# Two projections of a two-block layer as seven block products each, with head norms inside the key selection

## The chip, the cores and the metric

One core of one Trainium2 chip runs the kernel. The metric is device time in microseconds (us) of one execution. TensorE is called PE here, VectorE DVE, ScalarE ACT, GpSimd POOL, and the queue that issues most loads SP. They run side by side, and order between them is made by semaphores only.

## The reference, cut to what matters

Two transformer blocks run in sequence over 256 tokens of width 1024, all in float32. The change lies in the first attention of the first block.

```python
h = rms_norm(x, g_norm)
proj = h @ w_in                       # q_a, k_a, v_a, q_i, k_i, w_i, z_a, ... are column ranges of it
q_a = partial_rope(rms_norm(q_a.reshape(b, s, 8, 64), g_qn_a), cos_a, sin_a)   # k_a likewise
# dsa_attention(q_a, k_a, v_a, q_i, k_i, w_i):
dots  = einsum('bqhc,bsc->bhqs', q_i, k_i) * 64 ** -0.5
index = einsum('bhqs,bqh->bqs', relu(dots), w_i * 8 ** -0.5)      # causal
_, idx = lax.top_k(index, 64)         # each query keeps its 64 best keys
o_a = softmax(q_a k_a[idx] * 64 ** -0.5) v_a[idx]
```

Two more attentions (B and M), gates and an output projection follow, then the second block: two mixers, a cross attention, and a mixture of 32 experts whose weights are 201 MB.

## The kernel before

**Projections.** `h`, transposed, lies in `XT3` as 8 tiles of 128 rows by 256 tokens. The weights come in chunks of 512 columns (2 MB) from DRAM into three ring slots in turn, issued by SP when the last user of the slot is done. A chunk is multiplied in one of two ways. `project` (matmul on line 535) makes 16 matmuls 512 wide; each is two instructions in the trace, 32 for a chunk, and the result of both token tiles lies in one accumulator. `project_blocks` (lines 666 to 704, matmuls on lines 688 and 691) treats the chunk as a 2 by 2 block matrix and makes seven block products instead of eight (Strassen's scheme in Winograd's form): 28 matmuls 256 wide, 56 instructions. It needs four sums of weight blocks, which POOL makes (`weight_sums`, the `tensor_tensor` on line 1337, 16 steps of 128 by 256 for a chunk: 12 before the products, and four more once the second product is done), and four sums of `XT3`'s blocks, which POOL makes once, into `T_x`. DVE then joins the seven products (`combine`, lines 1897 to 1925) in four parts. Part k of the first three waits for product 2, 4 or 6; part 3 waits for product 7. The end of the third part frees the first accumulator, the end of the fourth part frees the second. In the kernel before, the chunks `mv`, `qi`, `qm`, the gates and most later ones are done so, while `qa`, `ka` and `va` (queries, keys and values of the first attention) go through `project`, and ACT copies their results out (`drain`, line 1458).

**Accumulators.** There are two, `ACC[0]` and `ACC[1]`, and every use takes the next one: use n waits until use n-2 has been freed (`acc`, line 495). `project` makes one use, `project_blocks` two, called low (products 1 to 4) and high (5 to 7).

**Order on PE** around the change: `qi`, `uq`, `ukv`, eight transposes, `qa`, `ka` (with the eight index score pairs of `dots`, line 783, one after each of its first eight matmuls), `va`, `za` (`project_t`, line 550), 16 transposes of `qa` and `ka`, `zb` with the first attention's steps in between, then `qm`.

**Order on DVE**: join `qi`; head norm of B's queries; head norm of B's keys (`norm_heads`: a reduce on line 1817, 12 small steps of a reciprocal root on lines 1767 to 1784, scale on 1826, gain on 1832); relu'd index scores times weights, added up (lines 2037 and 2039); mask (2047); the selection, eight rounds of `max` (2053) and `match_replace` (2056); two closing steps; then the head norm of `qa` and `ka` (`heads_normed` 4, called norm A here); then `silu_t` of `za` (line 1949), which waits for PE, and the attention.

**Order on POOL**: weight sums of `qi`; rope of the index queries; copies that join B's keys (1380, 1381), for which ACT waits to square them; rope of B's queries and keys (1322 to 1325) after B's key norm; rope of `qa` and `ka` after norm A; then the sums of `qm`.

**ACT** drains accumulators, squares heads for the norms, and takes the relu of the index scores. It may take pair n once DVE has added up pair n-2.

Of the kernel before, what the change touches and what calls it, by code (L numbers as in the profile page):

```python
# [20 lines left out]
ALU = mybir.AluOpType  # L21
# [5 lines left out]
S = 256  # L27
# [7 lines left out]
TOPK = 64  # L35
# [21 lines left out]
def two_block_layer(nc, A, out):  # L57
    ctx = ExitStack()
    with ctx:
# [126 lines left out]


        gate_chunks = [f"gate{n}{h}" for n in range(3) for h in range(2)]
        block_chunks = ["mv", "qi", "qm"] + gate_chunks + ["wout0", "wout1", "ckv0", "dq", "dk", "gv", "ckv1", "gg"]
        WS = slots[RING - 1]  # L190
        S_a, S_b = (WS[:, 1024 * i:1024 + 1024 * i].rearrange("p (k n) -> p k n", k=4) for i in range(2))
        T_x, T_mem2 = (t.rearrange("p (i k q) -> p i k q", i=4, k=4) for t in (WS[:, 2048:4096], R5[:, 2048:4096]))
# [220 lines left out]
        def keys_of(t):  # L413
            return P if t == 0 else S
# [79 lines left out]
        def _(pe):  # L494
# [20 lines left out]
            def project(name, lhs, k=KD, a=0, width=512, key=None, between=None, after=None, ready=None):  # L515


                if name != "mk":
                    wait_chunk(name)
                bank, full = acc(key or name)  # L520
                w = slot_of(name)
                for t in range(TT):
                    if t and between:
                        between()
                    for i in range(k):
                        if name == "mk":
                            if i % 4 == 0:
                                wait_drained(pe, ("mem", t, i // 4))
                            if t == 0 and i in (0, 2):
                                pe.wait_ge(first_landed[i // 2], 16)  # L530
                            elif (t, i) == (0, 4):
                                wait_chunk(name)
                        if ready and t == 0:
                            ready(i)
                        mm = nc.tensor.matmul(bank[:, t * 512:t * 512 + width], lhs[:, i, t * P:(t + 1) * P],  # L535
                                              w[:, i, a:a + width], start=(i == 0), stop=(i == k - 1))
                        if (t, i) == (TT - 1, k - 1):
                            mm.then_inc(full, 1)
                        if after:
                            after(t * k + i + 1, TT * k)  # L540
                last_job[name] = key or name
# [228 lines left out]
            for t in range(TT):  # L770
                turn(t, ("qi", t))
                turn(2 + t, ("ki", t))
            project("qa", XT3)
            for t in range(TT):
                wait_drained(pe, ("qi", t))
                wait_drained(pe, ("ki", t))
            def dots(n):
                t, h = n // 4, n % 4
                nk = keys_of(t)
                full = [aux(2 * (n % 2) + i, ("dots", n, i))[1] for i in range(2)]  # L780
                for i in range(2):
                    r = slice(64 * i, 64 * i + 64)
                    nc.tensor.matmul(AUX[2 * (n % 2) + i][:, 0:nk], QT4[r, h, t * P:(t + 1) * P], KIT[r, 0:nk],
                                     start=True, stop=True).then_inc(full[i], 1)

            project("ka", XT3, after=lambda done, total: dots(done - 1) if done <= 8 else None)
            project("va", XT3)
            project_t("za", XT3)
            pe.wait_ge(roped, 3)
            for t in range(TT):  # L790
# [488 lines left out]
        def _(pool):  # L1279
# [55 lines left out]
            def add_steps(out, a, b, op, counter, value):  # L1335
                for k in range(4):
                    ins = g.tensor_tensor(out[:, k, :], a[:, k, :], b[:, k, :], op)  # L1337
                ins.then_inc(counter, 1)
                pool.wait_ge(counter, value)

            def weight_sums(name):

                c = block_chunks.index(name)
                pool.wait_ge(slot_landed[slot_no[chunk_at[name]]], landed_value[chunk_at[name]])
                w = slot_of(name)
                w11, w12, w21, w22 = (w[:, 4 * j:4 * j + 4, 256 * i:256 * i + 256] for i in range(2) for j in range(2))
                if c:
                    pool.wait_ge(block_products, 3 * c - 1)
                add_steps(S_a, w21, w22, ALU.add, w_sums, 4 * c + 1)
                add_steps(S_b, S_a, w11, ALU.subtract, w_sums, 4 * c + 2)  # L1350
                add_steps(w21, w11, w21, ALU.subtract, w_sums, 4 * c + 3)
                pool.wait_ge(block_products, 3 * c + 1)
                add_steps(w12, w12, S_b, ALU.subtract, w_sums, 4 * c + 4)

            weight_sums("mv")
            for t in range(TT):
# [15 lines left out]
            for t in range(TT):  # L1372
                for i in range(2):
                    last = g.tensor_copy(EX[:, t * P + 64 * i:t * P + 64 * i + 64], PJ3[:, t, PJ_KI:PJ_KI + 64])
            last.then_inc(roped, 1)

            wait_drained(pool, "ukv0")
            wait_drained(pool, "ukv1")
            for t in range(TT):
                g.tensor_copy(KB[:, t, :, 0:64], KNB[:, t, :, :])  # L1380
                last = g.tensor_copy(KB[:, t, :, 64:96],
                                     PJ3[:, t, PJ_KR:PJ_KR + 32].unsqueeze(1).broadcast_to([P, 8, 32]))
            last.then_inc(kb_joined, 1)
            pool.wait_ge(heads_normed, 3)
            for t in range(TT):
                rope(heads(QB, t, 0, 8, 96), t, 64, 16, 1, 8)
                rope(KB[:, t, :, :], t, 64, 16, 1, 8)
            g.memset(SMALL[:, 72:73], 0.0).then_inc(roped, 1)
            pool.wait_ge(heads_normed, 4)
            for t in range(TT):  # L1390
                rope(heads(PJ3, t, PJ_QA, 16, 64), t, 0, 8, 2, 16)
# [36 lines left out]
        def _(act):  # L1428
# [25 lines left out]
            def drain(key, pairs):  # L1454

                bank = wait_full(act, key)
                for dst, src in pairs:
                    last = a_.activation(dst, src(bank), ACT.Copy)
                last.then_inc(free_sem(key), 1)

            def by_token(T3, c, width=512):
                return [(T3[:, t, c:c + width], lambda b, t=t: b[:, t * 512:t * 512 + width]) for t in range(TT)]
# [81 lines left out]
                drain(("ki", t), [(KIT[:, t * P:(t + 1) * P], lambda b: b[:, 0:P])])  # L1544
            act.wait_ge(kb_joined, 1)
            square_heads(R2[:, 0:1536], SQ[:, 0:1536], 96)
            drain("qa", by_token(PJ3, PJ_QA))
            for n in range(8):
                nk = keys_of(n // 4)
                if n >= 2:  # L1550
# [6 lines left out]
            wait_drained(act, "ka")  # L1557
            wait_drained(act, "qa")
            square_heads(PJ3[:, :, 0:1024], SQ[:, :].rearrange("p (t n) -> p t n", t=TT), 64)
            drain("va", by_token(PJ3, PJ_VA))  # L1560

            def tanh_of(key, dst, cols_=lambda b: b[:, :], done=None):

# [191 lines left out]
        def _(dve):  # L1755
# [3 lines left out]
            def link(ins):  # L1759
                steps[0] += 1  # L1760
                ins.then_inc(dve_steps, 1)
                dve.wait_ge(dve_steps, steps[0])
# [50 lines left out]
            def norm_heads(squares, groups, w, apply, n_gains):  # L1813

                sq_calls[0] += 1
                dve.wait_ge(squares_ready, sq_calls[0])
                v.tensor_reduce(MS[:, 0:groups], squares.rearrange("p (g w) -> p g w", g=groups), AX_X,
                                ALU.add).then_inc(squares_used, 1)
                dve.wait_ge(squares_used, sq_calls[0])
                rsqrt(groups, MS[:, 0:groups])  # L1820
                apply()
# [13 lines left out]
            def hv(ap, h):  # L1835
                return ap.rearrange("p (h w) -> p h w", h=h)
# [177 lines left out]
            def apply_heads(per_tile, gain, count=True):  # L2014

                for t in range(TT):
                    view, c = per_tile(t)
                    ins = scale_heads(view, c, view.shape[1])
                link(ins)
                for t in range(TT):  # L2020
                    view, c = per_tile(t)
                    ins = gain_heads(view, gain)
                ins.then_inc(heads_normed, 1)

            norm_heads(SQ[:, 0:1536], 16, 96, lambda: apply_heads(lambda t: (hv(QB[:, t, :], 8), 8 * t), GB_B), 1)
            norm_heads(SQ[:, 0:1536], 16, 96, lambda: apply_heads(lambda t: (KB[:, t, :, :], 8 * t), GB_B + 96), 1)

            for n in range(8):
                t = n // 4
# [18 lines left out]
            link(ins)  # L2048

            best = NW[:, 0:16].rearrange("p (t n) -> p t n", t=TT)  # L2050
            for k in range(TOPK // 8):
                for t in range(TT):
                    ins = v.max(best[:, t, :], IX3[:, t, 0:keys_of(t)])
                link(ins)
                for t in range(TT):
                    ins = v.match_replace(IX3[:, t, 0:keys_of(t)], best[:, t, :], IX3[:, t, 0:keys_of(t)], TAKEN)
                link(ins)
            for t in range(TT):
                nk = keys_of(t)
                ins = v.tensor_scalar(IX3[:, t, 0:nk], IX3[:, t, 0:nk], -2e38, NEG, ALU.is_gt, ALU.mult)  # L2060
            link(ins)
            for t in range(TT):
                nk = keys_of(t)
                ins = v.tensor_tensor(SEL3[:, t, 0:nk], IX3[:, t, 0:nk], causal[:, S - nk:S], ALU.add)
            link(ins)

            def apply_a(q, k, g0):
                def go():
# [14 lines left out]
                return go  # L2083

            norm_heads(SQ[:, :], 32, 64, apply_a(lambda t: hv(PJ3[:, t, 0:1024], 16), None, GB_A), 2)
            silu_t("za", ZT[:, 0:1024])
            attention("A", 0, 6)
            silu_t("zb", ZT[:, 1024:2048])
# [354 lines left out]
```

## Time and profile before

| | |
|---|---|
| median of 3 runs | 1104.6 us (1104.5 to 1105.12) |
| the profiled execution | 1104.28 us, of which the span of its trace 1102.5 us |
| PE busy | 921.5 us, 84% |
| DVE busy | 405.2 us, 37% |
| POOL busy | 244.4 us, 22% |
| ACT busy | 166.9 us, 15% |
| bytes moved | 290.38 MB, 263 GB/s over the span |

The profile is a page about one execution and a trace of it. Times in a trace count from the start of the span. Engines count as busy only with real work, and busy time is modelled for PE's pipelined matmuls, so the spacing of two starts is a better measure than a duration. A trace row of a timeline merges like instructions: start, time from the first start to the last end, line, operation, shapes, count, and in brackets how long the engine had been idle and what ended that.

### The profile page before, as it was taken

To read this page: it belongs to the slowest core of one execution; us is meant where nothing else is said; L and a number is where in the kernel's file an instruction comes from. 1 tells how busy PE (TensorE), PEld (TensorE's weight loads), DVE (VectorE), ACT (ScalarE), POOL (GpSimd) and SP (SyncE) were. 2 spreads that over 40 slices of the span, in tenths; PEclk is the share of its full clock that TensorE was granted. 3 is DMA by queue.
4 is the path that set the end of the run, shared out by engine and by line. 5 is a ranking of instruction groups with operands and counts; after the bars stand their busy time and mean duration, and the time that the engine had idled before them with its cause. 6 is when DMAs were issued, how large, how long until landed. Compare 5 with 4: busy or idle time off the path is not lost.

```text
span 1102.5 us, 12492 instructions
## 1 busy us (share of the span) xinstructions
PE 921.5 (84%) x5006; PEld 569.7 (52%) x5006; DVE 405.2 (37%) x994; ACT 166.9 (15%) x372; POOL 244.4 (22%) x366
## 2 busy tenths in 40 slices
PE   6999999999999999999999998757465566473757
PEld 3774487889999878864445653222222122131312
DVE  4736836663223746868445433010101001010101
ACT  2113223441001013013302230000000000000000
POOL 4442143044654958930000000000000000000000
PEclk9999999999999999999999999878878878687879
DMA  7645342232445344524419649999999999999996
GB/s 286 168 146 191 121 153 78 77 130 100 157 168 207 105 171 169 201 87 153 153 68 346 252 173 428 427 429 427 428 428 427 427 428 427 428 429 427 427 416 272
DMA packets 64328, 290.38 MB, mean 263 GB/s; under 512 B 9031, under 2 KB 11918, under 8 KB 51726
## 3 DMA queue, kind: packets, MB, share of 16 engines
q1 hardware_dynamic: 57840, 205.13, 48.6%
q10 hardware_dynamic: 6430, 84.44, 18.1%
q8 instruction: 41, 0.67, 0.3%
q14 instruction: 17, 0.14, 0.0%
HBM read 288.51 MB, written 1.05 MB: 263 GB/s over the span
## 4 chain that ended last, share of the span: by engine, by line
PE 62%; DMA 26%; DVE 6%; issue 2%; another core or an unknown queue 2%; ACT 2%; ACTq 0%; SPq 0%; DVEq 0%
DMA ring<-in_w_e_up_dram 12%; PE ACC L535 10%; PE ACC L691 10%; DMA BIG<-in_w_e_up_dram 9%; PE ACC L550 9%; PE PAIR L1086 8%; PE ACC L688 7%; PE ACC L574 5%; DMA PJ<-in_w_e_up_dram 4%; PE ACC L977 3%; PE PAIR L585 2%; PE PAIR L1117 2%; PE PAIR L662 1%; PE PAIR L639 1%
## 5 line engine op out<-in xcount | busy, mean ns | idle before, releaser
L1337 POOL TENSOR_TENSOR ring<-ring 128x256 f32<-128x256 f32 x272 | 205.3, 785 | 167.3 <-PE ACC L688 75.5
L1086 PE MATMUL PAIR<-ring,R 128*32 128x512 f32 x400 | 130.4, 708 | 41.2 <-DMA BIG<-in_w_e_up_dram 20.8
L550 PE MATMUL ACC<-BIG,ring 128*128 128x256 f32 (+1 forms) x464 | 103.8, 381 | 0.6 <-DVE R L1921 0.6
L550 PEld LDWEIGHTS ACC<-BIG,ring 128*128 128x128 f32 (+1 forms) x464 | 85.4, 187 | 15.5 <-issue 3.1
L2378 DVE SCALAR_TENSOR_TENSOR GB<-GB,PAIR 128x512 f32<-128x512 f32 x8 | 5.5, 688 | 231.8 <-ACT GB L1728 231.8
L1086 PE MATMUL PAIR<-BIG,R 128*32 128x512 f32 x176 | 62.8, 727 | 22.1 <-DMA PJ<-in_w_e_up_dram 22.1
L1086 PE MATMUL PAIR<-R 128*32 128x512 f32 x176 | 59.7, 695 | 25.0 <-DMA ring<-in_w_e_up_dram 12.5
L1117 PE MATMUL PAIR<-ring,BIG 128*32 128x512 f32 x160 | 64.5, 747 | 18.0 <-DMA R<-in_w_e_down_dram 12.4
L535 PE MATMUL ACC<-ring,BIG 128*128 128x512 f32 (+2 forms) x192 | 78.1, 559 | 0.5 <-DVE R L2214 0.5
L1086 PE MATMUL PAIR<-SQE,R 128*32 128x512 f32 x112 | 61.4, 711 | 17.0 <-DMA ring<-in_w_e_up_dram 10.7
L1086 PEld LDWEIGHTS PAIR<-ring,R 128*32 128x32 f32 x400 | 30.9, 128 | 73.2 <-issue 73.2
L691 PE MATMUL ACC<-ring 128*128 128x256 f32 x288 | 64.9, 381 | 1.9 <-ACT R L1512 1.0
L535 PE MATMUL ACC<-ring,R 128*128 128x512 f32 (+1 forms) x136 | 59.1, 584 | 0.7 <-DVE R L2007 0.4
L691 PEld LDWEIGHTS ACC<-ring 128*128 128x128 f32 x288 | 54.3, 190 | 10.4 <-issue 1.8
L1117 PE MATMUL PAIR<-PJ,BIG 128*32 128x512 f32 x128 | 46.7, 746 | 14.4 <-DMA ring<-in_w_e_down_dram 14.4
L2380 DVE SCALAR_TENSOR_TENSOR GB<-GB,PAIR 128x512 f32<-128x512 f32 x8 | 8.4, 1052 | 131.8 <-PE PAIR L1086 131.8
L574 PE MATMUL ACC<-ring,BIG 128*128 128x512 f32 x128 | 55.8, 592 | 0.0
L1086 PE MATMUL PAIR<-PJ,R 128*32 128x512 f32 x160 | 50.8, 698 | 5.7 <-DMA ring<-in_w_e_up_dram 5.0
L535 PEld LDWEIGHTS ACC<-ring,BIG 128*128 128x128 f32 x192 | 35.6, 190 | 35.2 <-issue 27.0
L688 PE MATMUL ACC<-ring 128*128 128x128 f32 x384 | 45.1, 276 | 0.0
L688 PEld LDWEIGHTS ACC<-ring 128*128 128x128 f32 x384 | 44.1, 192 | 0.7 <-issue 0.5
L691 PE MATMUL ACC<-ring,R 128*128 128x256 f32 x184 | 40.9, 379 | 0.0
(346 smaller groups left out, 1402.5 us busy)
## 6 DMA issues: line engine op xcount, KB each, us to landing
ring<-in_w_in_dram SPq DMA_DIRECT2D x20, 2048.0 KB, 7.9
ring<-in_w_e_gate_dram SPq DMA_DIRECT2D x8, 2048.0 KB, 40.1
ring<-in_w_e_up_dram SPq DMA_DIRECT2D x6, 2048.0 KB, 41.1
ring<-in_w_e_gate_dram ACTq DMA_DIRECT2D x6, 2048.0 KB, 26.5
ring<-in_w_e_down_dram SPq DMA_DIRECT2D x5, 2048.0 KB, 39.1
ring<-in_w_e_up_dram ACTq DMA_DIRECT2D x5, 2048.0 KB, 20.9
ring<-in_w_ckv_dram SPq DMA_DIRECT2D x4, 2048.0 KB, 8.0
BIG<-in_w_e_down_dram SPq DMA_DIRECT2D x4, 2048.0 KB, 22.9
```

What stands on the lines that cost most here:

```text
L535: mm = nc.tensor.matmul(bank[:, t * 512:t * 512 + width], lhs[:, i, t * P:(t + 1) * P], w[:, i, a:a + width], start=(i == 0), stop=(i == k ...
L550: mm = nc.tensor.matmul(bank[0:m, j * S:(j + 1) * S], w[:, i, a + j * P:a + j * P + m], rhs[:, i, :], start=(i == 0), stop=(i == k - 1))
L574: mm = nc.tensor.matmul(bank[:, c:c + 512], lhs[:, i, t * P:(t + 1) * P], w[:, i, :], start=(i == order[0]), stop=(i == order[-1]))
L585: mm = nc.tensor.transpose(bank[0:src.shape[1], j * P:(j + 1) * P], src, ident[:, :])
L639: mm = nc.tensor.transpose(bank[:, (j * heads + i) * P:(j * heads + i + 1) * P], e[:, i, j * P:(j + 1) * P], ident[:, :])
L662: mm = nc.tensor.matmul(bank[:, d * 256:(d + 1) * 256], value(j, h, d), p[:, j * 256:(j + 1) * 256], start=first, stop=last)
L688: mm = nc.tensor.matmul(bank[:, j * P:(j + 1) * P], left[:, k, j * P:(j + 1) * P], right[:, k, :], start=(k == 0), stop=(k == 3))
L691: mm = nc.tensor.matmul(bank, right[:, k, :], left[:, k, :], start=(k == 0), stop=(k == 3))
L977: mm = nc.tensor.matmul(ACC[t][:, h * 512:(h + 1) * 512], XT3[:, i, t * P:(t + 1) * P], slot_of(f"wco{h}")[:, i, :], start=False, stop=Fal ...
L1086: mm = nc.tensor.matmul(bank[r, :], M_xt[:, k, r], w[e][:, k, :], start=(k == 0), stop=(k == KD - 1))
L1117: mm = nc.tensor.matmul(AUX[2 + h][r, :], M_hidt[:, k, r], w[e][:, k, h * 512:(h + 1) * 512], start=(k == 0), stop=(k == 3))
L1337: ins = g.tensor_tensor(out[:, k, :], a[:, k, :], b[:, k, :], op)
```

## The change

`qa` and `va` are made by `project_blocks`. ACT's two drains of them go. POOL makes their weight sums: 12 steps for `qa` after the rope of the index queries, the other four after the copies that join B's keys; all 16 for `va` after the rope of B's queries and keys, ahead of that of `qa` and `ka`. DVE joins `qa` in two pieces, parts 0 to 2 between the two norms of B and part 3 after them. Norm A moves from behind the selection to behind its third round. Parts 0 to 2 of `va` come after norm A, part 3 after the sixth round. The index scores start four matmuls later within `ka`.

```diff
-        block_chunks = ["mv", "qi", "qm"] + gate_chunks + [...]
+        block_chunks = ["mv", "qi", "qa", "va", "qm"] + gate_chunks + [...]
 # PE
-            project("qa", XT3)
+            project_blocks("qa", XT3, T_x, x0_sums)
-            project("ka", XT3, after=lambda done, total: dots(done - 1) if done <= 8 else None)
-            project("va", XT3)
+            project("ka", XT3, after=lambda done, total: dots(done - 5) if 5 <= done <= 12 else None)
+            project_blocks("va", XT3, T_x, x0_sums)
 # POOL: weight_sums is split into first_sums (12 steps) and last_sum (4 steps)
             last.then_inc(roped, 1)
+            first_sums("qa")
...
             last.then_inc(kb_joined, 1)
+            last_sum("qa")
             pool.wait_ge(heads_normed, 3)
...
             g.memset(SMALL[:, 72:73], 0.0).then_inc(roped, 1)
+            weight_sums("va")
             pool.wait_ge(heads_normed, 4)
 # ACT
-            drain("qa", by_token(PJ3, PJ_QA))
-            drain("va", by_token(PJ3, PJ_VA))
 # DVE
             norm_heads(... QB ...)
+            combine("qa", by_rows(PJ3, PJ_QA), range(3))
             norm_heads(... KB ...)
+            combine("qa", by_rows(PJ3, PJ_QA), range(3, 4))
...
-            for k in range(TOPK // 8):      # the eight rounds, then the two closing steps, then norm A
+            select(range(0, 3))
             norm_heads(SQ[:, :], 32, 64, apply_a(lambda t: hv(PJ3[:, t, 0:1024], 16), None, GB_A), 2)
+            combine("va", by_rows(PJ3, PJ_VA), range(3))
+            select(range(3, 6))
+            combine("va", by_rows(PJ3, PJ_VA), range(3, 4))
+            select(range(6, TOPK // 8))
+            # the two closing steps
             silu_t("za", ZT[:, 0:1024])
```

## Rows read from the trace of the kernel before

**Rows 1.** The page: busy time, share of the span, instructions
```profile
PE 921.5 (84%) x5006; PEld 569.7 (52%) x5006; DVE 405.2 (37%) x994; ACT 166.9 (15%) x372; POOL 244.4 (22%) x366
```
**Rows 2.** A window of the end: us, busy per engine (instructions), granted clock, DMA share, GB/s
```profile
700.00:1102.00 402.00, 246.79 (x1651) 90.19 (x1649) 34.22 (x70) 15.82 (x29) 0.00 (x0) 0.81 0.99 417
```
**Rows 3.** Timeline of PE: qi's products, qa, the last dots, va, za
```profile
66.30 7.07 PE L691 MATMUL ACC<-ring 128*128 128x256 f32 x32
...
92.35 14.76 PE L535 MATMUL ACC<-ring,BIG 128*128 128x512 f32 x34
...
118.01 0.70 PE L783 MATMUL PAIR<-R 64*128 64x256 f32 x4
118.65 20.87 PE L535 MATMUL ACC<-ring,BIG 128*128 128x512 f32 x48
139.35 13.98 PE L550 MATMUL ACC<-BIG,ring 128*128 128x256 f32 x64
```
**Rows 4.** Timeline of DVE: joining qi, from part 0 to part 3
```profile
71.41 0.42 DVE L1913 COPY PJ<-ACC 128x256 f32<-128x256 f32 x1
...
73.41 0.42 DVE L1919 TENSOR_TENSOR PJ<-ACC,PJ 128x256 f32<-128x256 f32 x1 [0.33 <-PE ACC L691]
...
74.54 1.68 DVE L2007 TENSOR_TENSOR R<-PAIR,GC 128x384 f32<-128x384 f32 x4
76.23 0.42 DVE L1924 TENSOR_TENSOR PJ<-ACC,PJ 128x256 f32<-128x256 f32 x1
```
**Rows 5.** Timeline of DVE: B's key norm, score sums, mask, first round
```profile
97.70 1.75 DVE L1817 TENSOR_REDUCE MS<-SQE 128x16 f32<-128x1536 f32 x1 [2.36 <-ACT SQE L1452]
...
120.33 0.63 DVE L2047 TENSOR_TENSOR BIG<-BIG,MASKS 128x128 f32<-128x128 f32 x2
120.99 0.62 DVE L2053 MAX8 NW<-BIG 128x8 f32<-128x128 f32 x2
...
122.43 0.62 DVE L2053 MAX8 NW<-BIG 128x8 f32<-128x128 f32 x2
```
**Rows 6.** Timeline of DVE: norm A, first and last steps, and what comes next
```profile
133.63 2.29 DVE L1817 TENSOR_REDUCE MS<-SQE 128x32 f32<-128x2048 f32 x1
135.95 0.18 DVE L1767 TENSOR_SCALAR NW<-MS 128x32 f32<-128x32 f32 x1
...
138.63 2.36 DVE L1826 TENSOR_TENSOR PJ<-PJ,RS 128x1024 f32<-128x1024 f32 x2
141.03 2.50 DVE L1832 TENSOR_TENSOR PJ<-PJ,GB 128x512 f32<-128x512 f32 x4
154.42 1.22 DVE L1949 SCALAR_TENSOR_TENSOR BIG<-BIG,ACC 128x1024 f32<-128x1024 f32 x1 [10.90 <-ACT BIG L1565]
```
**Rows 7.** Timelines of POOL and DVE: a root step and a join beside sums
```profile
66.61 2.77 POOL L1337 TENSOR_TENSOR ring<-ring 128x256 f32<-128x256 f32 x4 [4.43 <-PE ACC L691]
...
67.39 0.65 DVE L1784 SCALAR_TENSOR_TENSOR NW<-NW 128x4 f32<-128x4 f32 x1
...
187.14 8.49 POOL L1337 TENSOR_TENSOR ring<-ring 128x256 f32<-128x256 f32 x12 [3.11 <-PE ACC L691]
...
191.92 0.42 DVE L1920 TENSOR_TENSOR PJ<-PJ,ACC 128x256 f32<-128x256 f32 x1
```
**Rows 8.** Timeline of POOL: rope of B, first step to last
```profile
105.78 0.73 POOL L1322 TENSOR_TENSOR BIG<-R,PJ 128x256 f32<-128x256 f32 x1 [9.62 <-DVE R L1832]
...
115.19 0.64 POOL L1325 TENSOR_TENSOR R<-BIG 128x128 f32<-128x128 f32 x1
```
**Rows 9.** Windows of 1 us, columns as in rows 2: PE stopped and started again
```profile
684.00:685.00 1.00, 0.40 (x4) 0.17 (x2) 1.00 (x3) 0.38 (x1) 0.00 (x0) 1.00 0.90 377
...
687.00:688.00 1.00, 0.00 (x0) 0.00 (x0) 0.00 (x0) 0.00 (x0) 0.00 (x0) 0.78 1.08 459
...
689.00:690.00 1.00, 0.02 (x4) 0.05 (x5) 0.00 (x0) 0.00 (x0) 0.00 (x0) 0.50 0.97 410
...
694.00:695.00 1.00, 1.00 (x12) 0.36 (x8) 0.00 (x0) 0.00 (x0) 0.00 (x0) 0.80 0.93 385
```

More of the change, by code:

```diff
@@ L188, in two_block_layer @@
         gate_chunks = [f"gate{n}{h}" for n in range(3) for h in range(2)]
-        block_chunks = ["mv", "qi", "qm"] + gate_chunks + ["wout0", "wout1", "ckv0", "dq", "dk", "gv", "ckv1", "gg"]
+        block_chunks = ["mv", "qi", "qa", "va", "qm"] + gate_chunks + ["wout0", "wout1", "ckv0", "dq", "dk", "gv", "ckv1", "gg"]
         WS = slots[RING - 1]
@@ L1339, in add_steps, with first_sums @@
                 pool.wait_ge(counter, value)
-            def weight_sums(name):
+            def first_sums(name):
                 c = block_chunks.index(name)
@@ L1351, in weight_sums, with last_sum @@
                 add_steps(w21, w11, w21, ALU.subtract, w_sums, 4 * c + 3)
+            def last_sum(name):
+                c = block_chunks.index(name)
+                w12 = slot_of(name)[:, 4:8, 0:256]
                 pool.wait_ge(block_products, 3 * c + 1)
                 add_steps(w12, w12, S_b, ALU.subtract, w_sums, 4 * c + 4)
+            def weight_sums(name):
+                first_sums(name)
+                last_sum(name)
             weight_sums("mv")
@@ L2050, in _, with select @@
             best = NW[:, 0:16].rearrange("p (t n) -> p t n", t=TT)
-            for k in range(TOPK // 8):
[L2052 to L2065, printed above, removed]
+            def select(rounds):
+                for k in rounds:
+                    for t in range(TT):
+                        ins = v.max(best[:, t, :], IX3[:, t, 0:keys_of(t)])
+                    link(ins)
+                    for t in range(TT):
+                        ins = v.match_replace(IX3[:, t, 0:keys_of(t)], best[:, t, :], IX3[:, t, 0:keys_of(t)], TAKEN)
+                    link(ins)
+            select(range(0, 3))
             def apply_a(q, k, g0):
@@ L2085, in _ @@
             norm_heads(SQ[:, :], 32, 64, apply_a(lambda t: hv(PJ3[:, t, 0:1024], 16), None, GB_A), 2)
+            combine("va", by_rows(PJ3, PJ_VA), range(3))
+            select(range(3, 6))
+            combine("va", by_rows(PJ3, PJ_VA), range(3, 4))
+            select(range(6, TOPK // 8))
+            for t in range(TT):
+                nk = keys_of(t)
+                ins = v.tensor_scalar(IX3[:, t, 0:nk], IX3[:, t, 0:nk], -2e38, NEG, ALU.is_gt, ALU.mult)
+            link(ins)
+            for t in range(TT):
+                nk = keys_of(t)
+                ins = v.tensor_tensor(SEL3[:, t, 0:nk], IX3[:, t, 0:nk], causal[:, S - nk:S], ALU.add)
+            link(ins)
             silu_t("za", ZT[:, 0:1024])
```

## The prediction

> **What bounds the kernel now.** I read the page first, then the windows, then the timelines of PE, DVE and POOL between 60 and 165 us. PE is busy for 84% of the span, DVE for 37%, POOL for 22% [rows 1]. From 700 us on the DMA engines are 99% busy, streaming expert weights [rows 2]. That stream starts when PE's chain has freed the buffers, so a microsecond won or lost on PE at 100 us should reach the end whole. Around the change PE runs without a gap: `qa` starts at 92.35, the last pair of index scores ends at 118.71, `za` starts at 139.35 [rows 3]. DVE has ended norm A at 143.53 and then idles 10.9 us until `za` is there [rows 6]. So PE bounds here, and DVE's slack is not needed by PE until the transposes after `za`.
>
> **What PE gains.** A plain chunk is 32 instructions. 48 of them fill 118.65 to 139.35, 0.431 us each, so 13.8 us a chunk [rows 3]. A block product chunk is 56 instructions. 32 of them take 7.07 us, tail included, so 6.91 us by starts, 0.216 us each, and the chunk takes 12.1 us [rows 3]. Two chunks: 3.4 us less on PE. If nothing waits the profiled 1104.3 us become 1100.9. ACT's two dropped drains are off the path.
>
> **What waits instead.** Count accumulator uses from 0 at `mk`: `qa` becomes uses 11 and 12, `ka` 13, `va` 14 and 15, `za` 16. `za` needs the accumulator of use 14, the low half of `va`, and DVE frees that by parts 0 to 2 of joining `va`. These stand in DVE's order behind norm A, and norm A behind three rounds of the selection. Before, `za` needed only `ka` drained by ACT. The question is when DVE gets there.
>
> 1. `qa` starts at 92.35 as before. Its sixth product, for which part 2 of the join waits, ends 48 instructions later, near 102.9. Queued behind that wait is B's key norm, which began at 97.70 [rows 5]. DVE then needs 1.1 us for part 2 (73.41 to 74.54 [rows 4]) and is at 104.0. The key norm takes 8.0 us: it ran from 97.70 [rows 5] until its gain released POOL, which started at 105.78 [rows 8]: 112.0. Part 3 takes 0.46 (76.23's row [rows 4], with its link): 112.5.
> 2. `ka` starts when `qa` ends, 92.35 + 12.1 = 104.4, against 106.15 before (92.35 + 13.8). With its scores it took 19.4 us, since `va`'s 13.8 before 139.35 leave 125.55. The last score pair ended at 118.71, 12.56 us after `ka`'s start, and now comes four matmuls (3.45 us) later: 120.4. The mask began 1.62 us after the last pair [rows 3, 5]: 122.0 now. DVE's own backlog, about 9 us of work from 112.5, ends at about the same time, so I take 122.3. The mask takes 0.66 us, a round 1.44 (120.99 to 122.43 [rows 5]), three rounds 4.3: 127.3. ACT has squared the heads by then (`ka` ends at 123.8, then about 3 us).
> 3. Norm A takes 9.9 us (133.63 to 143.53 [rows 6]): 137.2. Parts 0 to 2 take 2.8 us (71.41 to 74.54 less a wait of 0.33 [rows 4]): `za` could start at 140.0.
>
> PE is done with `va` at 104.4 + 19.4 + 12.1 = 135.9. So it stands idle for 4.1 us even with every DVE step at its old price, and the 3.4 us gained have turned into 0.65 us lost (140.0 against 139.35).
>
> **POOL's new work beside DVE.** Four small root steps beside weight sums started 0.68 us apart from 66.72 on (one of the four stands, 0.65 long [rows 7]), while alone the 12 steps from 135.95 to 138.63 are 0.22 apart [rows 6]. POOL itself was not slowed (2.77 us for four steps). A join step with only one input in SBUF kept its 0.42 beside sums [rows 7]. All 12 root steps of a norm are of this small kind. There are two places.
> - 12 steps for `qa`: the weights land about 84.1 and the steps end near 92.6 (8.49 us for 12 [rows 7]), over the root of B's query norm. This costs up to 3 us, hidden: DVE waits for `qa`'s sixth product until 102.9 anyhow. The copies for B's keys start within a microsecond of before. Were that cover gone, the 3 us would come through whole. The four later steps fit before product 7 starts.
> - 16 steps for `va`: they stand behind the rope of B, which starts when the key norm ends, 112.0, and takes 10.2 us (105.78 to 115.83 and a closing step of 0.1 [rows 8]): 122.2. Twelve steps at 8.5 us and four at 2.8 end at 133.5, at the worst spacing of the trace near 135. Norm A's root runs from 129.6 (127.3 and the reduce of 2.3). Until 133.5 it gets some six steps done at 0.68, the other six at 0.22: 2.7 us more, 3.5 if POOL ends at 135. I take 3.0. `va`'s own products get their sums in time (first at 125.1, wanted at 127.3); small delays of them would hide in PE's wait.
>
> `za` then starts at 143.0: 3.65 us later than before, after 7.1 us of idle PE. The rope of `qa` and `ka` on POOL (4.9 us) and the second half of the selection run under `za` (14 us); moving them costs nothing.
>
> **The clock.** In the trace PE stopped at 684.4 us, its granted clock fell from 2.4 to 1.2 GHz about 3 us later, stayed there when it started again at 689.98, and rose at about 694.4 [rows 9]. A stop of 7 us should do the same to `za`: some 3 to 6 us at half speed, of which half is lost, 1.5 to 3. I take 2.2, as in those rows. Should the clock not fall, it is 0.
>
> The sum: 1104.28 + 3.65 + 2.2 = 1110.1 for a profiled execution. The median of the runs lies 0.3 above the profiled one, so 1110.4.
>
> **What no row shows.** No `max` or `match_replace` ran beside POOL. Its cost in this company lies between nothing and the 0.45 more of a small step. At the upper end three rounds of 18 instructions take 8 us more, but then norm A runs after POOL is done and saves its 3: 5 us more in all. I take nothing, the end that the join step of rows 7 stands for: like it, each reads one tensor from SBUF. The Trainium skill ("VectorE: DVE Perf Modes", on two Vector instructions with no wait between them) counts the match instructions as one input each, and "SBUF — State Buffer" (practical consequences of the shared port) lets one-input instructions outside the two-port modes run free; by it the 5 us are 0. No run here shows it yet.
>
> **Rivals.**
> - *The joins are not late.* PE keeps its 3.4 us: 1101.2. For it speaks that DVE is 63% idle over the span; against it that DVE's steps from 102.9 to 140.0 are a chain each link of which has a row. It needs norm A and the join done 4 us sooner than their old durations allow. 7%.
> - *Late, but mildly.* POOL and DVE do not meet in norm A (sums over sooner, or steps that interleave), and a stop of 4 us brings the clock down for a short while only or not at all: +0.3 to +2.9, 1104.9 to 1107.5, middle 1105.9. 15%.
> - *Selection slowed by POOL*, as bounded above: 1115.4. It decides if a round takes 2.5 us or more instead of 1.44. 8%.
> - *Forecast*: `za` waits for the join of `va`, with both surcharges: 1110.4, own range 1107.5 to 1113.5. 70%.
>
> The range of 8 in 10 reaches from 1105.6 to 1114: part of the mild case, all of the forecast. A measurement of this kernel tells about 0.2% (2.2 us) from no change. Faster has the first rival, 0.07. Same (1102.4 to 1106.8) has most of the mild one, 0.12. Slower has the rest, 0.81.
>
> **What the profile after should show.** PE's stop in front of line 550 at about 136, some 7 us long, ended by DVE's join of `va`; no stop of note between 92 and 136. `qa` 12.1 us long. B's key norm at 104.0, first `max` at 123. Root steps of norm A at 0.65 us each while POOL is on line 1337, 0.2 after. The granted clock at 0.50 when `za` starts. The rest of the trace moved by one constant, about 6 us, up to the weight stream. The prediction is wrong if `za` starts with `va`'s last product, or if the clock stays at 1.00 through the stop (then about 1108.2), or if a later stage gives the delay back.

## The result

| | before | after |
|---|---|---|
| median | 1104.55 us (4 runs, 1103.96 to 1105.12) | 1111.25 us (4 runs, 1110.14 to 1112.16) |
| ratio to before | | 1.0061, 95% interval 1.0048 to 1.0073 |
| profiled execution, span | 1104.28, 1102.5 us | 1110.6, 1108.8 us |

The change makes the kernel 0.6% slower. The forecast was 1110.4 us with a range of 1105.6 to 1114. Two projections with an eighth of the matrix work taken out cost 6.7 us more, and the profile after shows where they go. First PE's timeline. It answers [rows 3]:

```profile
92.25 3.62 PE L691 MATMUL ACC<-ring,BIG 128*128 128x256 f32 x16
95.70 7.07 PE L691 MATMUL ACC<-ring 128*128 128x256 f32 x32
102.61 1.89 PE L691 MATMUL ACC<-ring,BIG 128*128 128x256 f32 x8
104.33 4.45 PE L535 MATMUL ACC<-ring,BIG 128*128 128x512 f32 x10
...
119.69 0.70 PE L783 MATMUL PAIR<-R 64*128 64x256 f32 x4
120.33 3.70 PE L535 MATMUL ACC<-ring,BIG 128*128 128x512 f32 x8
123.86 3.62 PE L691 MATMUL ACC<-ring,BIG 128*128 128x256 f32 x16
127.32 3.62 PE L691 MATMUL ACC<-ring 128*128 128x256 f32 x16
131.67 3.69 PE L691 MATMUL ACC<-ring 128*128 128x256 f32 x16 [0.73 <-issue]
135.20 1.89 PE L691 MATMUL ACC<-ring,BIG 128*128 128x256 f32 x8
143.63 15.76 PE L550 MATMUL ACC<-BIG,ring 128*128 128x256 f32 x64 [6.55 <-DVE PJ L1930]
159.23 1.91 PE L585 MATMUL PAIR<-ident,PJ 128*128 128x128 f32 x16
```

`qa` runs from 92.25 to 104.3, 12.1 us, and `va`'s products are done at 137.1. Then PE stands still for 6.55 us until `za` starts at 143.63, 4.3 us later than before. What releases it is line 1930 on DVE, the last operation of part 2 of the join of `va`. `za` itself takes 15.76 us instead of 13.98. The transposes behind it start at 159.23 instead of 153.16 (before), so 6.1 us are lost here, and the span is 6.3 longer.

DVE's timeline after shows what it did meanwhile. It answers [rows 5, 6]:

```profile
102.81 0.42 DVE L1928 TENSOR_TENSOR PJ<-ACC,PJ 128x256 f32<-128x256 f32 x1 [1.96 <-PE ACC L691]
...
103.94 1.74 DVE L1826 TENSOR_REDUCE MS<-SQE 128x16 f32<-128x1536 f32 x1
...
117.99 4.96 DVE L2050 SCALAR_TENSOR_TENSOR BIG<-SQE,SMALL,BIG 128x256 f32<-128x256 f32 x7
122.98 1.57 DVE L2058 TENSOR_TENSOR BIG<-BIG,MASKS 128x128 f32<-128x128 f32 x2
124.59 0.62 DVE L2065 MAX8 NW<-BIG 128x8 f32<-128x128 f32 x2
...
126.03 0.62 DVE L2065 MAX8 NW<-BIG 128x8 f32<-128x128 f32 x2
...
128.91 2.29 DVE L1826 TENSOR_REDUCE MS<-SQE 128x32 f32<-128x2048 f32 x1
131.23 0.38 DVE L1776 TENSOR_SCALAR NW<-MS 128x32 f32<-128x32 f32 x1
131.64 0.18 DVE L1777 TENSOR_SCALAR NWI<-NW 128x32 int32<-128x32 int32 x1
131.86 0.59 DVE L1778 TENSOR_SCALAR NW<-NWI 128x32 int32<-128x32 int32 x1
132.48 0.66 DVE L1787 TENSOR_TENSOR NW<-NW 128x32 f32<-128x32 f32 x1
133.17 0.65 DVE L1788 SCALAR_TENSOR_TENSOR NW<-NW 128x32 f32<-128x32 f32 x1
133.85 0.65 DVE L1793 SCALAR_TENSOR_TENSOR NW<-NW 128x32 f32<-128x32 f32 x1
134.54 0.19 DVE L1787 TENSOR_TENSOR NW<-NW 128x32 f32<-128x32 f32 x1
...
138.29 2.50 DVE L1841 TENSOR_TENSOR PJ<-PJ,GB 128x512 f32<-128x512 f32 x4
140.70 0.42 DVE L1922 COPY PJ<-ACC 128x256 f32<-128x256 f32 x1
...
143.07 0.42 DVE L1930 TENSOR_TENSOR PJ<-ACC,PJ 128x256 f32<-128x256 f32 x1
```

B's key norm starts at 103.94, behind the wait for `qa`'s sixth product. From there DVE works without a pause of note to 143.49, and the join of `va` is the last thing in the row. Norm A's root has 12 steps. Six of them start while POOL's sums run, and four of these six take 0.59 to 0.66 us (the other two 0.38 and 0.18); the six behind them take 0.19 each. POOL's row (its timeline after):

```profile
122.82 11.63 POOL L1337 TENSOR_TENSOR ring<-ring 128x256 f32<-128x256 f32 x16
```

The sums end at 134.45, and the next root step, at 134.54, is short.

### The profile page after: what moved, and what is told of

Same layout as the page of the kernel before. It is cut to its first block, busy times and chain, and to the rows that moved or that the text cites. A ratio compares the mean times of both kernels' runs of the same rounds, so it can differ in the third digit from the quotient of the medians.

```text
span 1108.8 us, 12645 instructions
## 1 busy us (share of the span) xinstructions
PE 918.6 (83%) x5054; PEld 579.9 (52%) x5054; DVE 421.3 (38%) x1010; ACT 164.9 (15%) x368; POOL 268.3 (24%) x398
## 3 DMA queue, kind: packets, MB, share of 16 engines
HBM read 288.51 MB, written 1.05 MB: 261 GB/s over the span
## 4 chain that ended last, share of the span: by engine, by line
PE 57%; DMA 27%; DVE 10%; issue 2%; ACT 2%; another core or an unknown queue 1%; ACTq 0%; SPq 0%; DVEq 0%
PE ACC L691 11%; DMA PJ<-in_w_e_down_dram 10%; PE ACC L550 9%; DMA PJ<-in_w_e_up_dram 9%; PE ACC L688 7%; PE ACC L535 6%; PE ACC L574 5%; PE PAIR L1086 5%; DMA ring<-in_w_e_down_dram 4%; PE PAIR L1117 4%; DMA ring<-in_w_e_up_dram 4%; PE ACC L977 2%; PE PAIR L585 2%; PE PAIR L662 1%
## 5 line engine op out<-in xcount | busy, mean ns | idle before, releaser
L1337 POOL TENSOR_TENSOR ring<-ring 128x256 f32<-128x256 f32 x304 | 230.2, 788 | 179.8 <-PE ACC L688 76.4
L691 PE MATMUL ACC<-ring 128*128 128x256 f32 x352 | 79.3, 381 | 3.1 <-issue 1.7
L691 PEld LDWEIGHTS ACC<-ring 128*128 128x128 f32 x352 | 66.4, 190 | 13.6 <-issue 2.9
L535 PE MATMUL ACC<-ring,BIG 128*128 128x512 f32 (+2 forms) x128 | 50.6, 542 | 0.4 <-DVE R L2233 0.4
L691 PE MATMUL ACC<-ring,BIG 128*128 128x256 f32 x192 | 44.8, 382 | 0.2 <-ACT BIG L1634 0.2
L688 PEld LDWEIGHTS ACC<-ring 128*128 128x128 f32 x384 | 44.1, 192 | 0.7 <-issue 0.5
```

The costliest lines, as they stand in the source:

```text
L688: mm = nc.tensor.matmul(bank[:, j * P:(j + 1) * P], left[:, k, j * P:(j + 1) * P], right[:, k, :], start=(k == 0), stop=(k == 3))
L691: mm = nc.tensor.matmul(bank, right[:, k, :], left[:, k, :], start=(k == 0), stop=(k == 3))
```

## The experiments

The theory on record says: `za` waits for `va`'s join because norm A stands ahead of it on DVE, POOL's sums make norm A longer, and the stop costs clock. All ratios below are to the kernel before.

### The join ahead of norm A

```diff
             select(range(0, 3))
-            norm_heads(SQ[:, :], 32, 64, apply_a(...), 2)
-            combine("va", by_rows(PJ3, PJ_VA), range(3))
             select(range(3, 6))
+            combine("va", by_rows(PJ3, PJ_VA), range(3))
+            norm_heads(SQ[:, :], 32, 64, apply_a(...), 2)
             combine("va", by_rows(PJ3, PJ_VA), range(3, 4))
```

> The changed kernel with one thing moved on DVE: rounds 3 to 5 of the selection, then parts 0 to 2 of joining va, and only then norm A. Theory (za waits for the join because norm A stands ahead of it): in the trace after, the join can follow the sixth round at 133.2 us and its part 2 ends near 136.5, before va's last product (137.1), so za starts near 137.1 instead of 143.6, PE has no stop, and the clock stays at 2.4 GHz. Norm A then runs from 136.5 beside an idle POOL, so its root steps are 0.22 us apart and it takes 9.9 us, to 146.5; the rope takes 4.9, to 151.4, about when za ends (150.9), so up to 0.6 us of wait there. Time: about 1.8 us under the kernel before, 1102.7, and 8 us under the changed kernel. Rival (the cost lies in the block products themselves, on PE or in POOL's sums, wherever norm A stands): as slow as the changed kernel within 2 us, 1109 to 1112.

Measured: 1102.91 us, ratio 0.9987 (0.9978 to 0.9996). PE's timeline of this kernel:

```profile
131.76 3.69 PE L691 MATMUL ACC<-ring 128*128 128x256 f32 x16 [0.73 <-issue]
135.29 1.89 PE L691 MATMUL ACC<-ring,BIG 128*128 128x256 f32 x8
137.02 13.98 PE L550 MATMUL ACC<-BIG,ring 128*128 128x256 f32 x64
151.77 1.97 PE L585 MATMUL PAIR<-ident,PJ 128*128 128x128 f32 x16 [0.78 <-POOL SMALL L1403]
```

The stop is gone with the same work on every engine. `za` follows `va`'s last product, and takes 13.98 us. Against the changed kernel the order of two items on DVE is worth some 8 us. The rival, that the block products cost by themselves, is out. The price forecast for the rope's wait, up to 0.6 us, was 0.78.

### PE kept busy through the stop

```diff
             project_blocks("va", XT3, T_x, x0_sums)
+            for i in range(2):
+                wait_drained(pe, ("dots", 6, i))
+            for _ in range(26):
+                nc.tensor.matmul(AUX[0][:, :], zeros_h[:, :], ..., start=True, stop=True)
```

> The changed kernel, with 26 matmuls of zeros (bf16, 512 wide, 0.216 us each, 5.6 us together) put on PE between va and za, into a bank that is free there. They lie inside PE's stop of 6.5 us, so za still starts at about 143.6. Theory (1.8 of the 6.3 us come from the clock, which fell to 1.2 GHz after the stop and stayed so for 3.5 us of za): the granted clock stays at 1.00 from 130 to 160 us, za's 64 instructions take 13.98 us instead of 15.76, and the kernel is 1.8 us faster than the changed one, 1109.4. Rival (za is long for another reason, such as late weights or DVE and POOL traffic): za stays at 15.8 us and the time at 1111.2.

Measured: 1109.1 us, ratio 1.0047 (1.0034 to 1.006). PE's timeline:

```profile
136.85 5.78 PE L791 MATMUL PAIR<-ones_h,zeros_h 128*128 128x512 bf16 x26
143.56 14.05 PE L550 MATMUL ACC<-BIG,ring 128*128 128x256 f32 x64 [0.93 <-DVE PJ L1935]
```

and two windows of 1 us, columns as in rows 2, first of the changed kernel, then of this one:

```profile
146.00:147.00 1.00, 1.00 (x4) 0.82 (x3) 0.93 (x4) 0.00 (x0) 1.00 (x2) 0.50 0.00 0
```

```profile
146.00:147.00 1.00, 1.00 (x6) 0.89 (x5) 0.93 (x5) 0.00 (x0) 1.00 (x2) 1.00 0.00 0
```

`za` starts at the same time, the granted clock stays at 2.4 GHz where it had been 1.2, and `za` is 1.7 us shorter. 5.8 us of useless matmuls make the kernel about 1.5 us faster (1.0047 against 1.0061, with intervals that overlap; the trace is the stronger evidence). So the clock's share of the loss is 1.7 to 1.8 us.

### Fewer sums on POOL

```diff
             def add_steps(out, a, b, op, counter, value):
-                for k in range(4):
+                for k in range(1 if 13 <= value <= 16 and counter is w_sums else 4):
```

This kernel leaves out three of the four steps of each of `va`'s sums, so its values of `va` are not the reference's, and its whole time may differ for that too. The stretch up to `za` is what counts.

> The changed kernel with three of four steps of va's weight sums left out on POOL (4 instead of 16), so that va's values are not those of the reference. POOL is done with them near 126 us instead of 134.5, before norm A's root. Theory (a small DVE step waits out a POOL step): norm A's root steps go back from up to 0.68 to 0.22 us apart, norm A takes 9.9 us instead of 11.8, the join of va ends about 1.9 us earlier, and za starts near 141.5 (PE's stop about 4.5 us, the clock still falls). Rival (POOL has nothing to do with it): norm A keeps 11.8 us and za starts at 143.6. The time over the whole may differ by more than that, since other values of va can change the routing of the experts; the stretch up to za is what counts.

Measured: 1108.61 us, ratio 1.0043 (1.0028 to 1.0057). DVE's timeline and PE's:

```profile
122.45 1.05 DVE L2058 TENSOR_TENSOR BIG<-BIG,MASKS 128x128 f32<-128x128 f32 x2
...
130.17 0.18 DVE L1776 TENSOR_SCALAR NW<-MS 128x32 f32<-128x32 f32 x1
...
132.63 0.19 DVE L1793 SCALAR_TENSOR_TENSOR RS<-NW 128x32 f32<-128x32 f32 x1
```

```profile
140.60 16.21 PE L550 MATMUL ACC<-BIG,ring 128*128 128x256 f32 x64 [5.01 <-DVE PJ L1930]
```

All 12 root steps are short now: 2.65 us from 130.17 to 132.82, against 4.63 from 131.23 to 135.86 in the changed kernel. Norm A takes 9.8 us, instead of 11.8. `za` starts at 140.60, 0.9 us earlier than expected: the mask, too, had waited for POOL (1.05 us now, 1.57 in the changed kernel, 0.63 before), and PE's scores were already 0.5 us earlier in this execution. The mask's 0.5 and the root's 2.0 are what this edit takes away of POOL's share, 2.5 us beside a stop of 6.55. PE still stops, for 5 us, and `za` still runs slow (16.21 us), so taking POOL's part away cures nothing by itself.

### qa alone

`va` is plain again, drained by ACT, without sums and joins; the rest is as in the changed kernel.

```diff
-            project_blocks("va", XT3, T_x, x0_sums)
+            project("va", XT3)
...
-            weight_sums("va")
-            combine("va", by_rows(PJ3, PJ_VA), range(3))
-            combine("va", by_rows(PJ3, PJ_VA), range(3, 4))
+            drain("va", by_token(PJ3, PJ_VA))
```

> The changed kernel with va as before: a plain product, drained by ACT, no sums of it on POOL and no joins on DVE. qa stays as block products, the norm stays inside the selection. Then za needs only ka's accumulator, which ACT drains at 125. Theory (qa's part is sound and its join is hidden; the loss comes from va's join alone): PE runs without a stop from 92 to za, which starts near 137.7, 1.7 us earlier than before, and the kernel takes 1102.9. Rival (qa's join already holds up PE or the index scores, or the extra DVE work costs by itself): no faster than the kernel before, 1104.5 or more.

Measured: 1102.86 us, ratio 0.9989 (0.998 to 0.9997). `za` starts at 137.46 with no stop (before: 139.35), and the transposes at 151.28 (before: 153.16), 1.9 us earlier. `qa`'s join is hidden as forecast, and so is the time by which POOL lengthens B's query norm. That is more than the 3 us of the forecast: the norm took 8.5 us before (86.87 to 95.34) and takes 12.5 here (86.63 to 99.13). The root pays 3.6 of it, and the gain step the rest, since `qa`'s last four sums run beside it (2.77 us instead of 2.31). In the changed kernel 1.96 us of DVE's wait for `qa`'s sixth product were left to cover it. The whole gains 1.2 us, not 1.7; the missing part is within the interval.

### The norm's move alone

The kernel before, with norm A behind the third round and nothing else changed.

```diff
+            select(range(0, 3))
             norm_heads(SQ[:, :], 32, 64, apply_a(...), 2)
+            select(range(3, TOPK // 8))
+            close_selection()
```

> The kernel before with one part of the change: norm A behind the third round of the selection instead of behind the eighth; no block products, no sums, no joins are added. Theory (the move is free while nothing behind norm A is wanted by PE before za ends): DVE does the same work in another order and ends it at the same 143.5 us, PE runs through, and the time is that of the kernel before, 1104, within 0.1%. Rival (the move brings or costs time by itself, since POOL's rope comes 7 us earlier and meets the last rounds): a difference of 1 us or more, 1103 or less or 1105 or more.

Measured: 1103.79 us, ratio 1.0003 (0.9994 to 1.0012). The move costs and brings nothing. DVE waits 3.67 us there for ACT's squares, so it ends this work at 147.1 and not at the 143.5 expected, but `za` starts at 139.37 as before.

### The norm last

The join-first kernel with norm A behind the whole selection, its old place.

```diff
             combine("va", by_rows(PJ3, PJ_VA), range(3))
-            norm_heads(SQ[:, :], 32, 64, apply_a(...), 2)
             combine("va", by_rows(PJ3, PJ_VA), range(3, 4))
             select(range(6, TOPK // 8))
...
+            norm_heads(SQ[:, :], 32, 64, apply_a(...), 2)
```

> The join-first kernel with norm A back behind the whole selection, where the kernel before had it. Theory: za still starts near 137.1 with no stop, but norm A ends near 151 and the rope near 156, while za ends at 150.9, so the stop of about 5 us stands ahead of the transposes now, and the clock falls again: the transposes start near 156 against 153.2 before, zb runs at half speed for some 3 us, and the time is 4 to 4.5 us above the kernel before, 1108.3. Rival (only the join's place matters, the norm's does not): as the join-first kernel, 1102.9.

Measured: 1110.1 us, ratio 1.0058 (1.0042 to 1.0073). PE's timeline:

```profile
136.78 13.98 PE L550 MATMUL ACC<-BIG,ring 128*128 128x256 f32 x64
156.48 3.52 PE L585 MATMUL PAIR<-ident,PJ 128*128 128x128 f32 x16 [5.73 <-POOL SMALL L1403]
159.84 5.35 PE L550 MATMUL ACC<-BIG,ring 128*128 128x256 f32 x24
```

The stop moves behind `za`, as forecast, and the transposes take 3.52 us instead of 1.91 at half clock. So DVE's order has two deadlines: the join by 137, norm A with its rope by about 151. The changed kernel misses the first, this one the second. The loss is 6.1 us by the medians, where 4 to 4.5 were expected. In the trace it is 4.9 us at line 688 (281.21 against 276.28 before): 3.3 from the later start of the transposes and 1.6 from their half clock. It is still 4.9 at the last expert products, and 5.2 between the two profiled executions (1109.44 against 1104.28). So nothing arises later in the trace; the rest lies between single executions and the median of only four, and its cause stays open.

### Both remaining waits taken out

```diff
 # DVE
-            select(range(3, 6))
+            select(range(3, 4))
+            v.tensor_reduce(MS[:, 0:32], ...)          # norm A's reduce
             combine("va", by_rows(PJ3, PJ_VA), range(3))
-            norm_heads(SQ[:, :], 32, 64, apply_a(...), 2)
+            rsqrt(32, MS[:, 0:32]); apply_a(...)()      # norm A's root and scaling
             combine("va", by_rows(PJ3, PJ_VA), range(3, 4))
-            select(range(6, TOPK // 8))
+            select(range(4, TOPK // 8))
 # POOL
-            pool.wait_ge(heads_normed, 3)
+            pool.wait_ge(heads_normed, 2)               # rope of B's queries
+            pool.wait_ge(heads_normed, 3)               # rope of B's keys, then va's sums
```

> The kernel of the join ahead of norm A, with what its trace still shows as lost taken out: the norm's reduce stands ahead of the join (four rounds, reduce, join of parts 0 to 2, root and scaling, part 3, four rounds), so that the rope of qa and ka is done 3 us earlier, and POOL ropes B's queries right after their own norm instead of behind the key norm, so that va's sums start 5 us earlier. Theory: the waits of 0.73 us (for va's third sum) and 0.78 us (for the rope) go, va ends near 136.4, za starts there or up to 0.4 later, the transposes follow it without a wait at about 150.2, and all of the 3.4 us of the block products are kept: 1.5 us faster than the join-first kernel, ratio to the kernel before 0.997, about 1100.7. Rival (the two waits only move, for instance into the closing steps of the selection or to DVE's score sums, which now have va's sums beside them): no better than the join-first kernel, ratio 0.9985 or more.

Measured: 1101.87 us, ratio 0.9978 (0.9969 to 0.9987). PE's timeline:

```profile
127.09 7.07 PE L691 MATMUL ACC<-ring 128*128 128x256 f32 x32
134.00 1.89 PE L691 MATMUL ACC<-ring,BIG 128*128 128x256 f32 x8
136.40 14.05 PE L550 MATMUL ACC<-BIG,ring 128*128 128x256 f32 x64 [0.51 <-DVE PJ L1932]
150.29 1.91 PE L585 MATMUL PAIR<-ident,PJ 128*128 128x128 f32 x16
```

Both waits are gone. 0.5 us is new in front of `za`, a part of what the rival said: the score sums have `va`'s weight sums beside them now and take 6.03 us for the last seven steps, instead of 4.96, so the join ends later than `va`. Still, the transposes start at 150.29, 2.9 us earlier than before and where they were expected. The time is 2.4 us under the kernel before and 9 us under the changed one; it is the fastest of the kernels here. It falls 0.8 us short of the ratio expected (0.997), at the edge of the interval.

## Why the prediction was right

**The gain on PE.** Forecast 3.4 us; `va` ended at 137.1 instead of the 135.9 forecast. 0.73 us are a wait inside it that I had ruled out. I had checked the first sum only. The third had no slack in my own numbers: done at 122.2 + 8.5 = 130.7, wanted 32 instructions into `va`, at 123.8 + 6.9 = 130.7. POOL's sums started 0.6 later than the 122.2 forecast (the rope took 10.7 us beside a busy DVE, not 10.2), the twelfth step ended at 131.57, and PE went on at 131.67. The wait hid in the stop, as the text had said it would, but it is real once the stop is gone, as the join-first kernel shows. Most of the other 0.4 us are no wait either: my sum went by starts, and at both stops the tail of the last instruction comes on top (0.17 us each, as 3.62 stands for 16 instructions that start over 3.45).

**The chain on DVE**, against the forecast:

| | forecast | after |
|---|---|---|
| B's key norm starts | 104.0 | 103.94 |
| score sums end | 122.3 | 122.95 |
| first `max` | 123.0 | 124.59 |
| three rounds | 4.3 | 4.3 |
| norm A | 12.9 (9.9 and 3.0) | 11.8 |
| join, parts 0 to 2 | 2.8 | 2.8 |
| `za` starts | 143.0 | 143.63 |

The term that was mis-sized is POOL's company, in its place more than in its size. I priced it for norm A alone, 3.0 us. The mask, two additions with both inputs in SBUF, paid 0.9 of it (1.57 us; 0.63 in the kernel with `qa` alone, where no sums run). The root paid 2.0 (4.63 instead of 2.65): it met 3.2 us of POOL's sums, not the 3.9 forecast, and its six steps there started 0.55 apart, not 0.68. That is 2.9 together. That the total came out at the 3.0 forecast is luck: an unpriced surcharge on the mask made up for a smaller one on the root.

The 0.6 us by which `za` started later than forecast come from the score sums. I had put DVE's backlog at "about 9 us of work from 112.5"; it took 10.7 (112.28 to 122.95, and with `qa` alone 112.15 to 122.84). Here, too, POOL was the company, with the rope of B: the steps of 256 columns take 0.71 us each beside it (4.96 for seven), where before, with POOL idle, they took 0.50 (the kernel before, a row of its DVE timeline):

```profile
117.61 1.00 DVE L2039 SCALAR_TENSOR_TENSOR BIG<-SQE,SMALL,BIG 128x256 f32<-128x256 f32 x2 [0.68 <-ACT SQE L1554]
```

The surcharge belongs to a stretch of time and to the operations in it.

**What no row had shown.** The rounds took 1.44 us beside POOL's sums (124.59 to 126.03), as alone [rows 5], so the lower bound of 0 was the right one. By the Trainium skill ("VectorE: DVE Perf Modes", on two Vector instructions with no wait between them) each match instruction has one input. No trace counts inputs, and the page's line does not name `max`; but the price of 0 that the prediction drew from it is what the trace shows for both, 1.44 us a round with and without company. The third rival is out.

**The clock.** Forecast 2.2 us, 1.5 to 3 as range; 1.78 in the trace (15.76 less 13.98), 1.7 by the kernel that kept PE busy. The windows after, of 1 us:

```profile
139.00:140.00 1.00, 0.00 (x0) 0.00 (x0) 1.00 (x2) 0.00 (x0) 0.00 (x0) 1.00 0.94 336
...
141.00:142.00 1.00, 0.00 (x0) 0.00 (x0) 0.93 (x4) 0.00 (x0) 1.00 (x2) 0.50 1.07 416
...
147.00:148.00 1.00, 1.00 (x5) 0.85 (x5) 0.96 (x5) 0.00 (x0) 1.00 (x3) 0.95 0.00 0
```

PE stopped at 137.1, the clock fell between 140 and 141, and rose again at 147, 3.5 us after the restart. That was 4.4 in [rows 9], hence the smaller loss. A shorter stop does not mean a smaller loss behind it. In the kernel with fewer sums PE stopped for 5.01 us only; its clock fell between 138 and 139, but stayed at 1.2 GHz for 4.4 us after the restart at 140.60, and `za` took 2.2 us more than 13.98:

```profile
144.00:145.00 1.00, 1.00 (x4) 0.73 (x4) 0.97 (x4) 0.00 (x0) 1.00 (x2) 0.51 0.00 0
145.00:146.00 1.00, 1.00 (x6) 0.90 (x5) 0.93 (x5) 0.00 (x0) 1.00 (x2) 1.00 0.00 0
```

**To the end of the kernel.** The forecast had 5.85 us at this point, 3.65 and 2.2; the trace has 4.28 and 1.78, together 6.1, so the two misses went opposite ways. 6.1 us at the transposes became 6.3 in the span and 6.7 in the medians. That the shift arrives whole was right for the changed kernel; for the small gains it holds only within about 1 us (1.9 us earlier at the transposes of the kernel with `qa` alone, 1.2 in the ratio). The tail from the first expert product on took 437.4 us before and 437.1 after, but 439.8 in the profiled execution of the fastest kernel. There PE was 2.8 us ahead of the kernel before at 645 and 0.45 ahead at the last expert product; at 1103.49 us it was also the slowest of that kernel's 11 executions. So one profile does not decide about a microsecond.

**The rivals.** "Not late" and "mildly late" failed for the same reason: with every step at its old price the join ends at 140.0, and the surcharges are facts. Without most of POOL's part PE still stopped for 5 us and the clock still fell and stayed low behind the restart, 4.4 us instead of 3.5 (the kernel with fewer sums, 1108.61 us), so the mild case ended nearer to the forecast than its 1104.9 to 1107.5.

## What to carry to other kernels

Before an accumulator is used twice as often, write down for each later user which engine now frees its bank, and everything that stands ahead of the freeing operation in that engine's queue; an engine that is busy 37% of the time can still be late where it counts. Place each item by its own deadline: here the join had to be done by 137 us and the norm with its rope by 151, and the order of just these two decided between 0.6% lost and 0.1% gained (0.2% with two small shifts more). And work added to POOL must be charged to every DVE operation of a slowed kind that runs in the same stretch, not only to the one that first comes to mind. Here these were operations with two inputs in SBUF, and `tensor_scalar` steps with one.

## What the runs showed of the hardware

- Beside POOL's two-input steps (0.69 to 0.73 us each) a small DVE step takes up to 0.66 us instead of 0.19, a mask of two additions 1.57 instead of 0.63. One input is no protection for `tensor_scalar`: in norm A's root two such steps took 0.38 and 0.59 us instead of 0.18, and the one between them 0.18. `max` and `match_replace` (1.44 us a round) and a reduce of 2048 columns (2.29 us) keep their times.
- It goes both ways: POOL's last four sums of `qa` took 4.59 us beside DVE's scaling and gain of 768 columns a step. The last four of `va` took 2.79 in the fastest kernel, beside rounds of the selection.
- After a stop of 6.55 us the granted clock was 1.2 GHz for the first 3.5 us of work, which cost 1.8 us; zero matmuls filling all but 0.93 us of the stop kept it at 2.4 GHz. After stops of 5.01 us (fewer sums) and 5.73 us (the norm last) the clock was at 1.2 GHz as well, and the work behind cost 2.2 and 1.6 us more.
